# Top-16 keys taken from SBUF as the scores are made, and one of eight expert rows added by VectorE: a hybrid S5 / convolution / PEER step on one core

## What is computed

```python
q = (xb @ w_q).reshape(128, 8, 2, 128)                 # 8 heads, two half queries
s1, s2 = q[:, :, 0] @ k1.T, q[:, :, 1] @ k2.T          # 128 keys each
v1, i1 = top_k(s1, 16); v2, i2 = top_k(s2, 16)
cand = v1[..., :, None] + v2[..., None, :]             # 16 x 16
sc, pos = top_k(cand, 16); eidx = i1 * 128 + i2 at pos
g = softmax(sc); act = gelu(sum_d u_tab[eidx] * xb)
out = sum over 8 heads x 16 of (g * act) * v_tab[eidx]
x = x + out
```

## Time and profile before

| | |
|---|---|
| median of 3 runs | 3440.96 us (3440.44 to 3450.82) |
| the profiled execution | 3443.49 us, its span 3441.4 us |
| TensorE busy | 3126.1 us (91%), granted clock 0.986 of full |
| VectorE / ScalarE / GpSimd busy | 2411.6 / 1216.7 / 1430.8 us |
| moved by DMA | 1327.99 MB, mean 386 GB/s |
| chain that ended last | PE 56%, DMA 24%, DVE 9%, issue 5%, ACT 4% |

### The profile page before, as it was taken

The page is one execution under the profiler, slowest core; times in us unless marked ns, Lnnn a source line. Parts: engine busy times, 40 slices in busy tenths (PEclk is TensorE's granted clock), DMA queues, the critical chain, the costliest instruction groups (busy, mean ns, idle before and its releaser), DMA issues.

```text
span 3441.4 us, 33582 instructions
## 1 busy us (share of the span) xinstructions
PE 3126.1 (91%) x10016; PEld 1785.2 (52%) x10016; DVE 2411.6 (70%) x5467; ACT 1216.7 (35%) x4072; POOL 1430.8 (42%) x1244
## 2 busy tenths in 40 slices
PE   7999999999999999999999999999998777777776
PEld 6777555555555555555654555655654222222232
DVE  7823798777656799776656799776656666766774
ACT  4223443343333443343334443342333333332332
POOL 1201455344344455343434454343444444444443
PEclk9999999999999999999999999999999999999999
DMA  4357999999999999999999999999999999999998
GB/s 135 94 176 282 393 405 402 419 415 419 418 412 418 393 398 406 418 416 412 414 414 420 415 394 414 418 412 417 412 417 403 420 419 419 404 419 410 420 399 345
DMA packets 227525, 1327.99 MB, mean 386 GB/s; under 512 B 25168, under 2 KB 46800, under 8 KB 88080
## 3 DMA queue, kind: packets, MB, share of 16 engines
q0 software_dynamic: 156672, 1140.92, 80.5%
q1 hardware_dynamic: 60688, 175.75, 13.7%
q10 hardware_dynamic: 9984, 9.18, 0.8%
HBM read 1306.73 MB, written 19.03 MB: 385 GB/s over the span
## 4 chain that ended last, share of the span: by engine, by line
PE 56%; DMA 24%; DVE 9%; issue 5%; ACT 4%; POOL 2%; SPq 0%; another core or an unknown queue 0%; POOLq 0%; ACTq 0%; DVEq 0%
PE ps_acc L758 31%; DMA rows<-in_experts,idx 23%; PE ps_a L589 14%; DVE rows L1395 4%; PE ps_a L665 4%; PE ps_v L589 3%; POOL rows L1565 2%; DMA sc<-score_rows 1%; DVE va L1241 1%; PE ps_a L692 1%; ACT coef L921 1%; PE ps_y L632 1%; ACT diag L925 1%; PE ps_a L669 1%; ACT uy L818 1%
## 5 line engine op out<-in xcount | busy, mean ns | idle before, releaser
L758 PE MATMUL ps_acc<-rows,diag 128*128 128x512 f32 x4352 | 2000.0, 608 | 268.1 <-ACT diag L925 262.2
L1565 POOL DMA_INDIRECT rows<-in_experts,idx x1088 | 1304.6, 1199 | 1732.7 <-PE ps_acc L758 1418.7
L1395 DVE CUSTOM_DVE_ANT_0 rows<-rows,xn 128x1024 f32<-128x1024 f32 x1088 | 1324.7, 1228 | 778.4 <-DMA rows<-in_experts,idx 763.5
L758 PEld LDWEIGHTS ps_acc<-rows,diag 128*128 128x128 f32 x4352 | 816.3, 193 | 1308.5 <-issue 855.0
L918 ACT ACTIVATE act_v<-dots 128x2 f32<-128x2 f32 x544 | 110.6, 203 | 1869.8 <-DVE dots L1395 1867.0
L925 ACT ACTIVATE diag<-pk,coef 128x128 f32<-128x128 f32 x1088 | 377.2, 394 | 17.7
L589 PE MATMUL ps_a<-xnT,ring 128*128 128x272 f32 x1536 | 370.7, 396 | 0.9 <-ACT xnT L806 0.7
L589 PEld LDWEIGHTS ps_a<-xnT,ring 128*128 128x128 f32 x1536 | 293.6, 192 | 91.6 <-issue 34.7
L921 ACT ACTIVATE coef<-act_v,soft 128x1 f32<-128x1 f32 x1088 | 261.4, 287 | 17.8
L1241 DVE SCALAR_TENSOR_TENSOR va<-va,pk 128x302 f32<-128x302 f32 x480 | 257.2, 600 | 1.9
L589 PE MATMUL ps_a<-gates,ring 128*128 128x272 f32 x1024 | 246.3, 394 | 2.2 <-ACT sig L892 1.3
(11 more groups left out here) (238 smaller groups left out, 1990.6 us busy)
## 6 DMA issues: line engine op xcount, KB each, us to landing
ring<-in_slabs SPq DMA_DIRECT2D x256, 512.0 KB
rows<-in_experts,idx POOLq DMA_INDIRECT x1088
ring<-made_slabs SPq DMA_DIRECT2D x24, 512.0 KB
sc<-score_rows SPq DMA_DIRECT2D x68, 128.0 KB
score_rows<-gp ACTq DMA_DIRECT2D x32, 256.0 KB
xt<-in_x_prompt SPq DMA_DIRECT2D x4, 1024.0 KB
out_y_prompt<-yt SPq DMA_DIRECT2D x8, 512.0 KB
ring<-made_slabs SPq DMA_DIRECT2D x12, 256.0 KB
```

Of the source, the lines that this page charges most:

```text
L758: ins = pe.matmul(ps_acc[:, h, :], diag[:, slot, :], rows[:, slot, D + h * 512:D + (h + 1) * 512], start=first, stop=False, skip_group_che ...
L1395: ins = dve.tensor_tensor_reduce(rows[:, slot, 0:D], rows[:, slot, 0:D], xn[:, :], 1.0, 0.0, ALU.mult, ALU.add, dots[:, s:s + 1])
L1565: pool.indirect_dma_start(out=rows[:, slot, :], out_offset=None, in_=experts, in_offset=bass.IndirectOffsetOnAxis(ap=idx[:, a, k:k + 1], a ...
```

## The change

The 16 best keys and their indices of each head, tile and key half (a *unit*, 32 a group) are now computed by VectorE straight from the SBUF copy of the score, in the half turns of a new table entry `tops`, and kept in `topv` and `topi`, now nine pairs deep. The prompt's stores to and loads from HBM go; the samples' 16 KB stores and the loads of 4 blocks for the last two pairs stay. ScalarE waits for `tops_done` where a buffer is used again. Pair 0 is chosen after half 56 of the opening. Separately, in pairs 0 to 23 the slot in ring place 7 goes, in turns 0 to 8 and 22 to 63 of each group, to VectorE: `x2t += coef * row`, with no diagonal and no matmuls. Such slots fall in odd turns: 4 + 21 a group, 75 in all. Place 7 has a semaphore of its own, `last_free`.

```diff
@@ OPENING @@
+     "tops": [52 + u // 2 for u in range(4 * HEADS)],
@@ STEADY @@
+     "tops": [97 + u for u in range(4 * HEADS)],
+REST = {"make": 4, "keep": 6, "square": 8, "mean": 9, "root": 10, "pass": 11, "tops": 1}
+CHOICE = 56
-        sc = sb("sc", [P, 2, 2 * KEYS])
-        topv = sb("topv", [P, 2, TOPK])
+        sc = gp[:, 0:4 * KEYS].rearrange("p (a c) -> p a c", a=2)
+        topv = sb("topv", [P, TOPS, 2, 2, TOPK])
...
+        def added(n, s):
+            k = PTURNS * (n % GPAIRS) + s // STEPS
+            return n < TILES * TPAIRS - GPAIRS and not 8 < k < 22 and s % RING == ADDED
...
@@ slots, TensorE @@
                 for s in range(s0, s1):
+                    if added(n, s):
+                        continue
...
@@ keep_scores, ScalarE @@
                 if m % 2 == 0 and h >= 2:
-                    act.wait_ge(score_out[b], 128 * g + 32 * (h // 2))
+                    act.wait_ge(score_out[b], 64 * g + 16 * (h // 2))
+                    act.wait_ge(tops_done, HEADS * g + h - 1)
...
-                    act.dma_start(sc_g[g, h], scsb[:, b, 0:2, :]).then_inc(score_out[b], 16)
                     act.dma_start(sc_s[g, h // 4, h % 4], scsb[0:NS, b, 2, :]).then_inc(score_out[b], 16)
...
@@ VectorE @@
+            def made_top(unit, g):
+                (head, f), t = divmod(unit // 2, 2), unit % 2
+                dve.wait_ge(a_done, A_BANKS + a_at(g, "score", 2 * head + f) + 1)
+                at, a = (GPAIRS * g + TPAIRS * t + head // 2) % TOPS, head % 2
+                key_top(scsb[:, a, t, f * KEYS:(f + 1) * KEYS], topv[:, at, a, f, :], topi[:, at, a, f, :])
+                if unit % 4 == 3:
+                    dve.sem_inc(tops_done, 1)
...
+            def add_slot(n, s):
+                dve.wait_ge(coef_done, PAIR * n + s + 1)
+                x2 = x2t[:, n // TPAIRS % 2, :]
+                mark(dve.scalar_tensor_tensor(x2, rows[:, ADDED, D:2 * D], coef[:, s:s + 1], x2, ALU.mult, ALU.add))
+                after(count[0])
+                dve.sem_inc(last_free, 1)
...
@@ a turn of VectorE @@
                 else:
                     dot(n, STEPS * r, STEPS * r + BATCH)
+                    if added(*earlier):
+                        add_slot(*earlier)
                     beside(2 * turn + 1)
                     dot(n, STEPS * r + BATCH, STEPS * (r + 1))
...
@@ SyncE @@
-                if r == 1 and n < LAST_PAIR:
-                    sp.wait_ge(score_used, 2 * n + 2)
-                    pass_wait()
-                    load_scores(n + 1, 1)
...
@@ gather, GpSimd @@
+                    if slot == ADDED:
+                        pool.wait_ge(last_free, rounds(n, s) + 1)
+                    else:
+                        pool.wait_ge(slot_free, (RING - 1) * rounds(n, s) + slot + 1)
```

More of the change, by code:

```diff
@@ L370, in program, with summed, rounds @@
         y_t = y_prompt.rearrange("b (t p) d -> (b t) p d", p=P)
-        sc_g = score_d[0:TILES * HEADS].rearrange("(g t h) p c -> g h p t c", g=GROUPS, h=HEADS)
-        sc_s = score_d[TILES * HEADS:BLOCKS].rearrange("k (f g p) c -> g f k p c", f=2, g=GROUPS)
+        sc_s = score_d.rearrange("k (f g p) c -> g f k p c", f=2, g=GROUPS)
+        def added(n, s):
+            k = PTURNS * (n % GPAIRS) + s // STEPS
+            return n < TILES * TPAIRS - GPAIRS and not 8 < k < 22 and s % RING == ADDED
+        summed_ahead = [0]
+        for n in range(LAST_PAIR + 1):
+            for s in range(PAIR):
+                summed_ahead.append(summed_ahead[-1] + (not added(n, s)))
+        def summed(n, s):
+            return summed_ahead[PAIR * n + s]
+        def rounds(n, s):
+            return PAIR // RING * n + s // RING
         def by_step(ap):
@@ L409, in rest_of, with late_tops @@
             return g if 0 <= g < GROUPS and h == REST[step] else None
+        def late_tops(g):
+            return [u for u, h in enumerate(plan(g).other["tops"]) if h >= (HALVES if g else OPEN + 2 * SKEW)]
         def ended_at(turn):
@@ L496, in _ @@
                 mix(h, 0)
[L498 to L504, removed]
             for turn in range(ALL_TURNS):
@@ L530, in _ @@
                         sp.dma_start(rst[half_tile, TILES % 2, :], rs_d[:, :]).then_inc(rs_in, 16)
-                if r == 1 and n < LAST_PAIR:
-                    sp.wait_ge(score_used, 2 * n + 2)
+                    sp.wait_ge(rest_sq, GROUPS)
                     pass_wait()
-                    load_scores(n + 1, 1)
[L535 to L538, removed]
+                    for a in range(2):
+                        sp.wait_ge(score_out[a], 64 * GROUPS)
+                        pass_wait()
+                    for a in range(2):
+                        load_scores(FIRST_SHARED, a)
+                if (n, r) == (FIRST_SHARED, 1):
+                    for a in range(2):
+                        sp.wait_ge(score_used, a + 1)
+                        pass_wait()
+                        load_scores(LAST_PAIR, a)
                 if turn > 32 and turn % 32 == 3:
@@ L1323, in mix @@
                     keep_rows(v_at(g, "rows", j), xt[0:NS, 2, :] if j else x2t[:, 0, :])
+                for unit in due("tops", h):
+                    made_top(unit, g)
                 if due("ms_next", h) and g < GROUPS - 1:
@@ L1376, in choose @@
                 a, p = divmod(r, PTURNS // 2)
[L1377 to L1382, removed]
+                if p < 2 and n >= FIRST_SHARED:
+                    shared_top(n, a, p)
+                if p == 2:
+                    pair_top(n, a)
+                if p == 3:
+                    experts_of(n, a)
             def weights(n):
@@ L1403, in beside @@
                     mix(*mix_half(number))
+                g = rest_of("tops", number)
+                if g is not None:
+                    for unit in late_tops(g):
+                        made_top(unit, g)
                 g = rest_of("keep", number)
@@ L1452, in _ @@
                 mix(h, 0)
-            for r in range(PTURNS):
-                choose(0, r)
+                if h == CHOICE:
+                    for r in range(PTURNS):
+                        choose(0, r)
             dve.wait_ge(norms_in, 16)
@@ L1464, in _ @@
                     weights(n)
+                earlier = (n, STEPS * r - 1) if r else (n - 1, PAIR - 1)
                 if turn % 32 == 0:
                     dot(n, STEPS * r, STEPS * (r + 1))
+                    if n and added(*earlier):
+                        add_slot(*earlier)
                     if ended_at(turn) is not None:
```

69 lines of the change are left out of this document (33 added, 36 removed).

## The result

The changed kernel took 3456.48 us (median of 8, 3451.2 to 3460.42) where the kernel before took 3446.05 beside it (8, 3440.44 to 3454.15): ratio 1.0026, 95% interval 1.0014 to 1.0038. So it is slower by 5 to 9 us; 15 us of gain had been forecast.

A forecast was written before the change was run, and what follows sets the result against it. The DMA's rate was taken as the bound, TensorE just under it, VectorE over it in 13 turns of 64. Terms -14 - 18 + 7 + 10 = -15 us on 3443.5 gave 3428.5, at the median 3426; range 3396 to 3465.

The forecast's parts named there:

- Part 3: Windows: all 32 units of a group in 16 turns; 192.5 us against 190.3, a loss of 7 us in all.
- VectorE may fall about 7 us behind before the DMA runs dry: Windows: rows queue for 5 to 11 us, so that much lateness of VectorE's 199.5 us is absorbed.
- Rival (b): Windows: VectorE becomes the bound, waits 3.2 us per score, not 2.3; window 213 us, time 3466; chance 0.26.
- Place 7 is now freed after two dots of the next turn: Ring place 7: its release comes about as late as TensorE's, so it costs nothing.
- Part 5: Additions: 75 slots leave TensorE (131 us in all), worth nothing at the present rate because the DMA covers it.
- Part 1: Traffic: 42.7 us of score stores and loads go; 7.6 in each window, 14 us elsewhere a straight gain.
- Part 2: Steep turns: 14.7 us of choices leave VectorE; 177.3 becomes 171.3 us, 6 us a group, 18 gained in all.
- by its share 174.7: Steep turns: the time the DMA wants for a set going by its share, beside 170.5 by its rate.
- Part 4: Opening: units delay the first index to 302 and turn 3's end by 17.7 us; 10 us lost.
- rows landed and unread: Opening: about three rows, 2.9 us each, make the transfers only 9 us late where dots are 17.7 late.
- (a): Windows: the rows' queue covers VectorE's stops and the DMA's rate holds, Part 3 becomes -23, time 3396; chance 0.24.
- (c): Mixing turns: TensorE was the bound, so the additions pay, up to 131 us; time 3310; chance 0.04.

The follow-up runs named there:

- e12: The changed kernel once more with nothing altered, in the last job: 3456.45 us, ratio 1.0015 to the kernel before.
- e1: The changed kernel without its additions, all slots staying on TensorE: 3450.68 us, ratio 1.0006 to the kernel before.
- e14: The changed kernel with the addition and `end` behind two dots, not four, in each tile's first turn: 3448.81 us, ratio 0.9992.
- e4: The kernel before with VectorE's additions alone, scores still going through HBM: 3442.47 us, ratio 0.9987.
- e5: The changed kernel with steady units one half turn later and no additions by VectorE: 3431.63 us, ratio 0.9932.
- e2: The changed kernel with every steady unit one half turn later (98 in place of 97), opening unchanged: 3425.09 us, ratio 0.9932.
- e11: e7 with additions only in turns 4 to 8 and 22 to 49 of a group: 3417.53 us, ratio 0.9893.
- e7: e2 with the opening split: VectorE takes the second tile's 16 units later, in turns 0, 1 and 4 to 11: 3415.4 us, ratio 0.9892.
- e9: e7 with the addition and `end` behind two dots, not four, in each tile's first turn: 3408.36 us, ratio 0.9871.
- e6: e2 with two unused 512-element passes added on VectorE in each of the 16 turns of each window: 3447.76 us, ratio 0.9988.

## Why the prediction was wrong

By e12 against before: turns to the eighth +13.9 us, steep turns -15.7, windows +23.5, the rest -6.2, in all +15.5 by the traces (about +5 by the ratio; see above for the gap). The forecast had +10, -18, +7, -14.

**Part 3, the windows, is where it failed: 16.5 of the 30.5 us.** Against the changed kernel's first trace it is 12.9 of 22.7 us, with 11.2 more in the rest. The wait was sized well: 15 waits with 25.5 us left were forecast, 14 with 22.2 came; without additions the forecast's sum was 34.5, and e1 has 30.9 in 14 waits. So was VectorE's sum: 199.5 us forecast, 196.0 and 198.4 measured in a window in which it hardly waits for rows. Two steps failed.
- "VectorE may fall about 7 us behind before the DMA runs dry", for free. It was read from the time that a gather takes to land, which is a queue of transfers and not a stock of unread rows. With VectorE last, the window simply became its sum: 5.6, 4.5 and 9.8 us over before's three windows in place of 2.2 each, and 8.0, 5.5 and 10.0 in e12. Rival (b) named this mechanism, but with a longer wait and windows of 208 us; waits of 2.4 us at most and windows of 194 to 198 were enough, because the gain elsewhere did not come in full either.
- "Place 7 is now freed after two dots of the next turn." In the first turn of a tile it is four; the diff shows it. There GpSimd stood 6.4 us and TensorE 4.4. The price of that order in the changed kernel, with `end`, is the 7.6 us of e12 against e14. The additions' "nothing" of Part 5 came out as a loss of 3 to 7 us (e1 against the changed kernel); that the order is its reason is likely but not shown, for e4 has the same stops and a small gain.

**Part 1.** 7.6 us of traffic in each window: q10's part came, 6.1 us; even in e5, with VectorE out of the way, the three windows took 568.0 us, no less than before's 565.6; in the first one the gathers took up more. So no run had the window's gain in full. The "straight gain" of 14 us elsewhere is 13.4 in e5 and 15.2 in e2, whose units come late enough, but 6.2 in e12 and 2.8 in the changed kernel's first trace, whose units do not. So it is straight only where the windows before it do not leave VectorE late; how that carries over was not taken apart.

**Part 2, steep turns: right.** 171.3 us was forecast for a full set in place of 177.3; 170.9 and 168.5 came (e12: 170.5 and 171.1), and e1 with 172.7 and 170.9 shows that the selection alone does it. The term "by its share 174.7" does not follow from the shares as printed (177.3 x 1.00 / 1.02 is 173.8), which would move the forecast by half a microsecond. VectorE's 152.7 us is above the 148 forecast.

**Part 4, the opening.** The chain of steps was right, at the clock it was made for: first index 302 (e2 302.0), turn 0's dots done at 332.2 (333.2), turn 3's end 17.7 us late (20.4 in e2, 20.1 in e12). Wrong was to halve it for "rows landed and unread": at turn 8 13.9 us of e12 were left, 17.5 of e2's, in place of 10. (The changed kernel's first trace has 10.8 there, with the 4.8 us of the faster opening in it.)

**Part 5.** "At the present rate that buys nothing": e5 against e2 and e11 against e7 agree within their intervals, in kernels where VectorE has time.

**Rivals.** (a) needed VectorE's stops hidden; e2 has none, one half turn later, but its windows (572.8 us) stay over before's too. (c) is out: with TensorE's 75 slots gone (e4) the time fell 4 us. The Trainium skill, "DMA: Bandwidth & Descriptors", section "Where 436 GB/s comes from", puts the ceiling at 435.2 GB/s. The traces do not reach it: no 40th of any profiled span here was above 421, with the DMA share between 0.98 and 1.02 in every 100 us of the last stage from 2700 to 3300.

The fault was thus in the slack that was taken for granted and in one order, not in the path that was described: the same selection, one half turn later, its opening cut in two and the tile's end reordered, is 1.3% faster than the kernel before (e9).

## What to carry to other kernels

An engine that works in order should not be given a result in the same step in which a neighbour makes it, if that neighbour waits for the engine's own last output: one step later cost nothing that these traces show and took 30 us off. The latency of a transfer in a full queue is no slack for its consumer; slack is the time in which the consumer is seen to wait for rows (e2's 17.2 us a window), and a load of known size (e6) shows that there is no more. When a semaphore's release moves to another engine, walk through every branch of that engine's loop, the rare turns first.

## What was not expected of the hardware

TensorE's clock fell behind its stop for `yt`. Around the tile's end in e12 (same columns as above):

```profile
1102.00:1106.00 4.00, 4.00 (x22) 3.24 (x20) 3.72 (x10) 0.00 (x0) 0.94 (x1) 1.00 1.03 423
1106.00:1110.00 4.00, 0.24 (x2) 0.00 (x0) 4.00 (x7) 1.99 (x8) 0.00 (x0) 0.90 0.99 410
1110.00:1114.00 4.00, 1.96 (x3) 0.93 (x4) 3.58 (x11) 1.91 (x5) 0.94 (x1) 0.50 0.45 132
1114.00:1118.00 4.00, 4.00 (x9) 1.73 (x8) 3.68 (x11) 0.00 (x0) 1.14 (x1) 0.75 0.55 225
```

TensorE stood 5.80 us for `yt`, the granted clock went to 0.50, the 1.2 GHz level, and when work came back it ran its first microseconds at half rate, with the DMA at 132 and 225 GB/s beside it. The last slow weight load and the first fast one:

```profile
1115.62 0.34 PEld L771 LDWEIGHTS ps_acc<-rows,diag 128*128 128x128 f32 x1 [0.52 <-issue]
1116.24 0.19 PEld L771 LDWEIGHTS ps_acc<-rows,diag 128*128 128x128 f32 x1 [0.28 <-issue]
```

In the kernel before, TensorE stood 1.99 us at the same place, with clock 1.00 and 410 GB/s; over the first window the clock was 1.00 before, 0.96 after, 0.93 in e12. It is TensorE's stop that counts, not VectorE's lateness: in e1, with VectorE as late, the clock stayed at 1.00 over that window; in e4, with VectorE waiting for rows, TensorE stood 4.49 us and the clock was 0.72 in the 4 us around the stop's end. e4's windows were no longer for it. What the fall costs apart from the wait itself was not measured in a late window.

And an execution's opening differs by 4 to 6 us with the clock granted between 100 and 200 us, 0.93 or 0.98, whatever the kernel. A single trace's first dot can't be compared closer than that.
